# mLSTM gate exponentials for the queries, split into a rounded and a remaining part

## The chip, the cores and the metric

The kernel runs on one core of one Trainium2 chip. The metric is the device time of one execution in microseconds (us), the median of a few runs of the same program. Engines are called as the profile calls them: PE (TensorE matmuls), PEld (TensorE weight loads), DVE (VectorE), ACT (ScalarE), POOL (GpSimd), SP (SyncE, which starts DMAs here).

## The reference, cut to what matters

One step of two trunk layers of a streaming encoder for 512 prompt frames and 8 streams of 16 frames. In each layer an FFN, three parallel token mixers (MLA attention, mLSTM, HGRN2), an output projection and another FFN follow one another. The change touches the mLSTM, of which this is the part that counts:

```python
def step(carry, inp):                       # one chunk of L frames, 4 heads
    c, n, m = carry
    qc, kc, vc, lic, lfc = inp
    b = jnp.cumsum(lfc, axis=1)
    ...
    log_inter = b + m[:, None, :]
    m_t = jnp.maximum(log_inter, jnp.max(logw, axis=2))
    w_intra = jnp.exp(logw - m_t[:, :, None, :])
    w_inter = jnp.exp(log_inter - m_t)
    qk = jnp.einsum('bthd,bshd->btsh', qc, kc) * w_intra
    num = jnp.einsum('btsh,bshv->bthv', qk, vc) + w_inter[..., None] * jnp.einsum('bthd,bhdv->bthv', qc, c)
```

`w_inter` is one number for each head and frame, and it scales the queries `qc` of that head. All inputs and outputs are float32.

## The kernel before

The 640 frames (512 and 8 x 16) lie along the free dimension, as five tiles of 128 (`TILES` 5; tiles 0 to 3 are the prompt, `PT_` is 4). Each layer runs the FFN, the projection, `mla`, `recurrent`, `wout` and the second FFN. Every engine has its own program, written out by hand in the order in which it runs; waits on semaphores join them. Nothing is scheduled by a program: what stands earlier in an engine's code runs earlier.

**The attention loop (`mla`)** runs over 32 steps, n = 4 h + i, of 8 heads h and 4 query blocks i. In a step PE multiplies scores (L1157), DVE sets the masked corner and takes the maximum (`maximum(n)`: L2675, L2676), ACT takes the exponential with that maximum (`probabilities(n)`), PE transposes the result (L1166), ACT copies it back, and PE multiplies with the values (L1176). Scores run two steps ahead, so `maximum(21)` is needed by ACT's exponential of step 21, and that by PE's transpose of step 21. Between the steps each engine does other work of the layer:

- DVE computes the mLSTM gates of the 4 heads, on 4 partitions by 640 frames, one function ahead of the maximum of each of steps 5 and 8 to 16. `gate_starts_exponents` (step 14) leaves the logarithm of `w_inter` in `UB[0:4, 0, :]`. `gate_negative` (step 16) writes `NBR`, 64 rows high: it sets 64 rows to zero (L2766), writes the negated maximum, rounded to the type fp32r, into rows 0 to 3 (L2767), and what the rounding left into rows 32 to 35 (L2768). At step 20 DVE also multiplies a pair of heads' output (`pair_output`, L2688), after `maximum(20)`.
- ACT takes the gate exponentials at step 17 (`gates_exp`, L1936 to L1943), the last of them in place in `UB[0:4, 0, :]`, and then raises `ge_sb`. All of ACT's activations are recorded on line L1539, the helper.
- POOL works through the taps of the convolution (`tap_of`): two multiplications (L3216, L3217, one input from SBUF each) and an addition (L3219, two inputs from SBUF), over and over. After the taps it clears `QPE` and stores two states from `GB`; ACT waits for these stores ahead of `stream_keys(0)`.

After the loop PE runs `pair_rows` (L1187) and a few filling matmuls (L869), waits for ACT's `kn_sb`, and begins the attention of the streams (L1226). There ACT turns constants into fp32r for the mLSTM (`MASKR`, `SELR`, `IDR`, event `mr_sb`).

**The recurrent part (`recurrent`)** runs `front(t)` for the five tiles, each between the output and update products of earlier tiles. `front` multiplies masks and gate rows (L1336, L1338), queries with keys (L1351), transposes the keys of two head pairs g (L1354) and, for t = 1 to 4, spreads the four rows of `w_inter` over the 128 rows of a head pair: `SELG[:, g, :]` holds ones at the rows that belong together, and the product (L1356) is made in plain float32 with all 128 rows of `SELG` and of `UB[:, 0, cut]`. DVE then reads bank 1 of PSUM for the weighted keys `KW` (L2900) and bank 2 for the weighted queries `QG` (L2906).

Of the kernel before, what the change touches and what calls it, by code (L numbers as in the profile page):

```python
# [119 lines left out]
def shape_constants():  # L120

    inv = (10000.0 ** (-np.arange(0, ROPE, 2, dtype=np.float32) / ROPE)).astype(np.float32)
    pos = np.concatenate([np.arange(TP), np.tile(PAST + np.arange(TS), NSEQ)]).astype(np.float32)
    ang = inv[:, None] * pos[None, :]
    rope = np.concatenate([np.cos(ang)] * 2 + [-np.sin(ang), np.sin(ang)]).astype(np.float32)
    swap = np.zeros((P, P + ROPE), np.float32)
    for j in range(ROPE):
        swap[NOPE + (j + ROPE // 2) % ROPE, QK + j] = 1.0
        swap[[NOPE + j, QK + j], P + j] = 1.0
    s, t = np.arange(P)[:, None], np.arange(P)[None, :]  # L130
    causal = np.where(s <= t, 0.0, -FAR)
    streams = np.where((s <= t) & (s // TS == t // TS), 0.0, -FAR)
    masks = np.stack([causal, streams], axis=1).astype(np.float32)
    level = np.zeros((P, NLEV, P), np.float32)
    for n, h in enumerate(LEVELS):
        level[:, n] = (s // (2 * h) == t // (2 * h)) & (s % (2 * h) < h) & (t % (2 * h) >= h)
    level[:, NLEV - 1] = s == t
    starts = np.zeros(T, bool)
    starts[0:TP:P] = True
    starts[TP::TS] = True  # L140
    going = np.broadcast_to(1.0 - starts.astype(np.float32), (P, T))
    drop = np.zeros((MH, T), np.float32)
    drop[:, TP::TS] = -FAR
    select = np.zeros((P, MH, P), np.float32)
    for h in range(MH):
        select[[h, 32 + h], h] = 1.0
    pair = np.zeros((P, 2, P), np.float32)
    for h in range(MH):
        pair[h, h // 2, 64 * (h % 2):64 * (h % 2) + 64] = 1.0
    owner = (np.arange(P)[:, None] // TS == np.arange(NSEQ)[None, :]).astype(np.float32)  # L150
    return {"c_rope": rope, "c_swap": swap, "c_mask": masks, "c_level": level.astype(np.uint8),
            "c_going": np.ascontiguousarray(going), "c_drop": drop, "c_select": select, "c_pair": pair, "c_owner": owner,
            "c_ident": np.eye(P, dtype=np.float32), "c_ones": np.ones((P, P), np.float32)}
# [35 lines left out]
def encoder(nc, A, O):  # L189
# [51 lines left out]
    LVL = tile(ctx, "lvl", [P, NLEV, P], U8)  # L241
    AT = tile(ctx, "at", [P, TILES, 2, 2, P])
    QK1 = tile(ctx, "qk1", [P, 2, T])
    SELG = tile(ctx, "selg", [P, 2, P])
    GB = tile(ctx, "gb", [P, 2, T])
    s_w = ExitStack()
    tile(s_w, "gap_nbr", [P, T])
    NBR = tile(s_w, "nbr", [P, T], F32R)
    s_w.close()
    UB = tile(ctx, "ub", [P, 2, T])  # L250
# [215 lines left out]
    ext_sb, conv_sb, csilu_sb = event("ext_sb", 1), event("conv_sb", 2), event("csilu_sb", 2)  # L466
    tap_sb = event("tap_sb", 4)
    ga_sb, gl_sb, ge_sb, gt_sb = steps("gates_act", 4)
    gab_sb, gd_sb = steps("gates_dve", 2)
    gt_ps, oexp_sb, msk_sb = (event(n, 1) for n in ("gt_ps", "oexp_sb", "msk_sb"))  # L470
    mr_sb, qm_sb, cd_sb, sd_sb = (event(n, 1) for n in ("mr_sb", "qm_sb", "cd_sb", "sd_sb"))
    qg_sb = event("qg_sb", TILES - 1)
# [261 lines left out]
    def _(pe):  # L734
# [592 lines left out]
        def recurrent(l):  # L1327

            def front(t):
                cut = slice(t * P, (t + 1) * P)  # L1330
                if t:
                    pe.wait_ge(*wexp_sb.nth(l, t - 1))
                else:
                    pe.wait_ge(*mr_sb.nth(l, 0))
                mask = MASKR[:, t // PT_, :].unsqueeze(1).broadcast_to([P, MH, P])
                pe.matmul(PS[:, 0, :], IDR[:, :], mask, start=True, stop=False, skip_group_check=True)  # L1336
                for h in range(MH):
                    mm = pe.matmul(PS[:, 0, h * P:(h + 1) * P], SELR[0:64, h, :], NBR[0:64, cut],  # L1338
                                   start=False, stop=True, skip_group_check=True)
                mm.then_inc(nb_ps.sem, 1)  # L1340
                if t == 0:
                    pe.wait_ge(*csilu_sb.nth(l, 1))
                    pe.wait_ge(*spt_sb.nth(l, NSEQ - 1))
                else:
                    pe.wait_ge(*wt_sb.nth(l, t - 1))
                    pe.wait_ge(*kw_sb.nth(l, t - 1))
                    if t >= 2:
                        pe.wait_ge(*qg_sb.nth(l, t - 2))
                for h in range(MH):
                    rows = slice(64 * (h % 2), 64 * (h % 2) + 64)  # L1350
                    pe.matmul(PS[:, 1 + h % 2, h // 2 * P:h // 2 * P + P], QKC[rows, 2 + h // 2, cut],  # L1351
                              QKC[rows, h // 2, cut], start=True, stop=True)
                for g in range(2):
                    pe.transpose(PS[:, 1, 256 + g * P:256 + (g + 1) * P], QKC[:, 2 + g, cut], IDENT[:, :])  # L1354
                    if t:
                        pe.matmul(PS[:, 2, 256 + g * P:256 + (g + 1) * P], SELG[:, g, :], UB[:, 0, cut],  # L1356
                                  start=True, stop=True)
                if t:
                    pe.wait_ge(*kdt_sb.nth(l, t - 1))
                else:  # L1360
                    pe.wait_ge(*kd_sb.nth(l, 1))
                    pe.wait_ge(*mla_done.nth(l, 0))
                for g in range(2):
                    mm = pe.transpose(PS[:, 3, g * P:(g + 1) * P], KDF[:, g, cut], IDENT[:, :])
                mm.then_inc(mk_ps.sem, 1)
# [169 lines left out]
    def _(act):  # L1535
# [337 lines left out]
        def mla(l):  # L1873
# [62 lines left out]
            def gates_exp():  # L1936
                act.wait_ge(*gd_sb.nth(l, 0))
                act.wait_ge(*ml_zero.nth(l, 0))
                run(G3[64:68, :], GB[0:MH, 0, :], ACT.Exp, scale=-1.0)
                run(G3[96:100, :], GB[0:MH, 1, :], ACT.Exp)  # L1940
                run(WIE[:, 0:PT_], UB[0:MH, 0, ENDS_P], ACT.Exp)
                chain.link(run(WIE[:, PT_:12], UB[0:MH, 0, ENDS_S], ACT.Exp))
                run(UB[0:MH, 0, :], UB[0:MH, 0, :], ACT.Exp).then_inc(ge_sb.sem, 1)  # L1943

            def gate_columns():
                act.wait_ge(*gt_ps.nth(l, 0))
# [82 lines left out]
            for b in range(NSEQ):  # L2029
                if b + 2 < NSEQ:  # L2030
                    stream_keys(b + 2)
                if 1 <= b <= 3:
                    decays(l, b + 3)
                if b + 1 < NSEQ:
                    stream_transposed(b + 1)
                if b + 2 < NSEQ:
                    stream_exp(b + 2)
                if b == 0:
                    act.wait_ge(ml_in, 16 + (l + 1) * 64)
                    run(MASKR[:, :, :], MASK[:, :, :], ACT.Copy)  # L2040
                    run(SELR[:, :, :], SEL[:, :, :], ACT.Copy)
                    run(IDR[:, :], IDENT[:, :], ACT.Copy).then_inc(mr_sb.sem, 1)
                if b == 4:
                    act.wait_ge(*conv_sb.nth(l, 1))
                    run(QE[:, :, :], BC[:, :, :], ACT.Exp)
                if b == 5:
                    act.wait_ge(*kd_sb.nth(l, 0))
                    run(KDF[:, :, :], KDF[:, :, :], ACT.Exp)
                    run(EBL[:, :, 0:PT_], BC[:, :, ENDS_P], ACT.Exp)
                    run(EBL[:, :, PT_:12], BC[:, :, ENDS_S], ACT.Exp).then_inc(qe_sb.sem, 1)  # L2050
# [158 lines left out]
    def _(dve):  # L2209
# [450 lines left out]
        def mla(l):  # L2660
# [99 lines left out]
            def gate_ends_exponents():  # L2760
                for cut, n0, n1, w in GATE_CUTS:
                    rows = lambda ap: ap.rearrange("h (n t) -> h n t", t=w)
                    V.tensor_tensor(rows(GB[0:MH, 1, cut]), rows(G3[0:MH, cut]), spread(GE[:, n0:n1], w), ALU.subtract)

            def gate_negative():
                chain.link(V.memset(NBR[0:64, :].bitcast(F32), 0.0))  # L2766
                chain.link(V.tensor_scalar(NBR[0:MH, :], g, -1.0, None, ALU.mult))  # L2767
                V.scalar_tensor_tensor(out=NBR[32:32 + MH, :], in0=g, scalar=-1.0, in1=NBR[0:MH, :].bitcast(F32),  # L2768
                                       op0=ALU.mult, op1=ALU.subtract).then_inc(gd_sb.sem, 1)
# [12 lines left out]
            for n in range(NT):  # L2782
# [19 lines left out]
                    gate_ends_exponents()  # L2802
                if n == 16:
                    gate_negative()
                if n % PT_ == PT_ - 1 and n // PT_ + 1 < H:
                    rotated(n // PT_ + 1, 1)
                maximum(n)
# [76 lines left out]
        def recurrent(l):  # L2884
            dve.wait_ge(*gt_sb.nth(l, 0))

            def weights(t):
# [10 lines left out]
                if t >= 2:  # L2898
                    dve.wait_ge(*upd_ps.nth(l, t - 2))
                V.scalar_tensor_tensor(out=KW[:, t % 2, :, :],  # L2900
                                       in0=PS[:, 1, 256:512].rearrange("p (h d) -> p h d", d=DK),
                                       scalar=DK ** -0.5, in1=spread(GT[:, t, 96:100], DK),
                                       op0=ALU.mult, op1=ALU.mult).then_inc(kw_sb.sem, 1)
                if t:
                    cut = slice(t * P, (t + 1) * P)
                    V.tensor_tensor(QG[:, :, cut], PS[:, 2, 256:512].rearrange("p (g t) -> p g t", t=P),  # L2906
                                    QKC[:, 0:2, cut], ALU.mult).then_inc(qg_sb.sem, 1)

            def mlstm_out(t):
# [417 lines left out]
```

## Time and profile before

| | us |
|---|---|
| median of 3 runs | 2605.98 (2605.72 to 2606.77) |
| the profiled execution, its own time | 2605.07 |
| its span, first to last instruction | 2603.3 |
| PE busy | 2562.1 (98%) |
| DVE busy | 1637.9 (63%) |
| ACT busy | 1145.4 (44%) |
| POOL busy | 533.4 (20%) |

Between the span and the execution's own time lie 1.77 us, outside the instructions. The granted TensorE clock is 0.999 of full speed over the span. The stages that the change touches lie, in layer 0, at 617 to 706 us (attention loop), 706 to 764 us (attention of the streams) and 764 to 804 us (recurrent), and in layer 1 some 1283 us later. The chain of waits, followed back from the last instruction, tells which engine's work the end waits for at each moment; the timeline shows what each engine does at that time and how long it stood idle before.

### The profile page before, as it was taken

The numbers are of one execution on the slowest core, as the hardware profiler recorded it, in microseconds if no ns is written. First come the engines' busy times: TensorE is split into PE (matmuls) and PEld (weight loads), VectorE is DVE, ScalarE is ACT, GpSimd is POOL, SyncE is SP. The second block draws the span as 40 slices with busy tenths as digits, with TensorE's granted clock in tenths as the row PEclk, the third lists the DMA queues.
The fourth block names the chain that finished last, engine by engine and source line by source line (L and its number), as shares of the span: only waits on it lengthen the run. The fifth ranks groups of instructions, "written<-read, shape, count | busy, mean of one in ns | idle before, by whom it ended". The sixth has DMA issues, their size and how long they took to land.

```text
span 2603.3 us, 44569 instructions
## 1 busy us (share of the span) xinstructions
PE 2562.1 (98%) x17872; PEld 2446.5 (94%) x17872; DVE 1637.9 (63%) x2534; ACT 1145.4 (44%) x1946; POOL 533.4 (20%) x440
## 2 busy tenths in 40 slices
PE   9999999999999999999999999999999999999998
PEld 8999999996689999999999999999956899999998
DVE  5666575646465866657577574765564757757473
ACT  5343344424654534334454342553165635434253
POOL 0010112103754101011210110121066441101011
PEclk9999999999999999999999999999999999999999
DMA  3322324220025122332313222334000261322321
GB/s 116 90 81 81 97 65 113 73 59 11 20 54 100 49 82 81 85 94 71 108 33 97 82 71 76 88 90 105 27 11 29 46 130 33 97 81 71 88 83 59
DMA packets 369794, 190.73 MB, mean 73 GB/s; under 512 B 38541, under 2 KB 365536, under 8 KB 369630
## 3 DMA queue, kind: packets, MB, share of 16 engines
q1 hardware_dynamic: 365248, 177.89, 25.3%
q0 software_dynamic: 4000, 10.47, 1.7%
q8 instruction: 108, 1.77, 0.3%
q14 instruction: 56, 0.46, 0.1%
q10 hardware_dynamic: 382, 0.14, 0.0%
HBM read 182.53 MB, written 5.93 MB: 72 GB/s over the span
## 4 chain that ended last, share of the span: by engine, by line
PE 91%; DVE 3%; POOL 2%; ACT 2%; issue 1%; DMA 1%; SPq 0%; DVEq 0%; POOLq 0%; ACTq 0%
PE ps L737 27%; PE ps L739 27%; PE ps L738 27%; PE ps L1114 2%; POOL misc L3216 1%; POOL qkc L3219 1%; PE ps L1125 1%; PE ps L1226 1%; DVE at L2711 1%; PE ps L1227 1%; PE ps L1157 0%; PE ps L1248 0%; ACT css L1539 0%; PE ps L1176 0%; PE ps L1239 0%
## 5 line engine op out<-in xcount | busy, mean ns | idle before, releaser
L737 PE MATMUL ps<-xh,w 128*128 128x320 f32 x1920 | 595.1, 310 | 3.1 <-DVE css L2976 3.1
L739 PE MATMUL ps<-xh,w 128*128 128x320 f32 x1920 | 593.3, 309 | 0.0
L738 PE MATMUL ps<-xl,w 128*128 128x320 f32 x1920 | 593.2, 309 | 0.0
L1539 ACT ACTIVATE w<-raw 128x512 fp32r<-128x512 f32 (+3 forms) x372 | 315.8, 861 | 483.9 <-PE ps L739 466.2
L3073 POOL TENSOR_TENSOR hl<-ub,hh 128x640 fp32r<-128x640 f32 x88 | 174.2, 1980 | 1448.1 <-ACT hh L1539 1380.9
L737 PE MATMUL ps<-hh,w 128*128 128x320 f32 x1408 | 438.0, 311 | 3.3 <-DVE ub L2367 1.2
L739 PE MATMUL ps<-hh,w 128*128 128x320 f32 x1408 | 435.0, 309 | 0.0
L738 PE MATMUL ps<-hl,w 128*128 128x320 f32 x1408 | 435.0, 309 | 0.0
L737 PEld LDWEIGHTS ps<-xh,w 128*128 128x128 f32 x1920 | 360.4, 188 | 5.3 <-DVE css L2976 3.6
L738 PEld LDWEIGHTS ps<-xl,w 128*128 128x128 f32 x1920 | 360.4, 188 | 0.3
L739 PEld LDWEIGHTS ps<-xh,w 128*128 128x128 f32 x1920 | 360.4, 188 | 0.0
L737 PEld LDWEIGHTS ps<-hh,w 128*128 128x128 f32 x1408 | 264.2, 188 | 8.4 <-issue 8.0
L737 PE MATMUL ps<-tc,w 128*128 128x320 f32 x864 | 267.0, 309 | 0.0
L738 PE MATMUL ps<-tc,w 128*128 128x320 f32 x864 | 267.0, 309 | 0.0
L739 PE MATMUL ps<-tc,w 128*128 128x320 f32 x864 | 267.0, 309 | 0.0
L738 PEld LDWEIGHTS ps<-hl,w 128*128 128x128 f32 x1408 | 264.3, 188 | 0.5
L739 PEld LDWEIGHTS ps<-hh,w 128*128 128x128 f32 x1408 | 264.3, 188 | 0.0
L2378 DVE TENSOR_TENSOR y<-ps,y 128x640 f32<-128x640 f32 x83 | 68.4, 824 | 261.9 <-PE ps L739 261.9
L2242 DVE TENSOR_TENSOR w<-raw,w 128x512 fp32r<-128x512 f32 (+1 forms) x216 | 180.4, 863 | 3.9 <-ACT w L1539 3.9
L739 PEld LDWEIGHTS ps<-tc,w 128*128 128x128 f32 x864 | 162.2, 188 | 0.0
L737 PEld LDWEIGHTS ps<-tc,w 128*128 128x128 f32 x864 | 162.2, 188 | 0.0
L738 PEld LDWEIGHTS ps<-tc,w 128*128 128x128 f32 x864 | 162.2, 188 | 0.0
(420 smaller groups left out, 4674.4 us busy)
## 6 DMA issues: line engine op xcount, KB each, us to landing
raw<-in_w_ffn_in_dram SPq DMA_DIRECT2D x176, 512.0 KB
raw<-in_w_ffn_out_dram SPq DMA_DIRECT2D x192, 192.0 KB
raw<-in_w_in_dram SPq DMA_DIRECT2D x38, 512.0 KB
raw<-in_w_ffn_out_dram SPq DMA_DIRECT2D x64, 128.0 KB
wraw<-in_w_out_dram SPq DMA_DIRECT2D x8, 512.0 KB
raw<-in_w_out_dram SPq DMA_DIRECT2D x8, 512.0 KB
out_dram<-xio SPq DMA_DIRECT2D x5, 512.0 KB
xin<-in_x_prompt_dram SPq DMA_DIRECT2D x4, 512.0 KB, 7.6
```

The source lines that it names most:

```text
L737: pe.matmul(out, wh, xh, start=first, stop=False, skip_group_check=loose)
L738: pe.matmul(out, wh, xl, start=False, stop=False, skip_group_check=loose)
L739: return pe.matmul(out, wl, xh, start=False, stop=last, skip_group_check=loose)
L1114: mm = pe.matmul(PS[:, 6 + h % 2, at:at + w], k_, q_, start=True, stop=True)
L1125: mm = pe.matmul(PS[:, half, 0:HALF], WUQ[:, c, h, :], CQ[:, c, half * HALF:(half + 1) * HALF], start=c == 0, stop=c == 1)
L1226: pe.matmul(PS[:, 4, :], ql, CT[:, b % 2, :], start=True, stop=False)
L1227: pe.matmul(PS[:, 4, :], qp, KPT[:, b % 2, 0:PAST], start=False, stop=True)
L1539: return nc.scalar.activation(out, in_, func, **kw)
L2242: V.tensor_tensor(lo, group_raw(n, q % 2), hi.bitcast(F32), ALU.subtract)\
L2378: ins = V.tensor_tensor(y, ps, y, ALU.add) if add else V.tensor_copy(y, ps)
L2711: ins = V.copy_predicated(out, mask, new)
L3073: G.tensor_tensor(HL[:, k, :], UB[:, j, :], HH[:, k, :].bitcast(F32), ALU.subtract).then_inc(hl_ready.sem, 1)
```

## The change

The spread of `w_inter` is made from two parts in fp32r instead of from one row in float32. The exponential goes to `R[0:4, :]` instead of in place. A new function on DVE, `gate_parts`, stands ahead of the maximum of step 21: it waits for ACT's exponentials, clears 64 rows of `UBR` (which lies on the same memory as `UB[:, 0, :]`), writes the rounded exponential into rows 0 to 3 and the remaining part into rows 32 to 35. ACT makes an fp32r copy of `SELG` (in place), beside the other constants. `SELG` has ones at rows h and 32 + h. PE multiplies 64 rows of `SELGR` with 64 rows of `UBR`, both heads' products ahead of the two key transposes, into bank 1; the transposes go to bank 2, and DVE reads the two banks accordingly. At tile 1 PE waits for `gx_sb`, which `gate_parts` raises.

```diff
@@ shape_constants
-        pair[h, h // 2, 64 * (h % 2):64 * (h % 2) + 64] = 1.0
+        pair[[h, 32 + h], h // 2, 64 * (h % 2):64 * (h % 2) + 64] = 1.0
@@ encoder, tiles
+    s_w = ExitStack()
+    SELGR = tile(s_w, "selgr", [P, 2, P], F32R)
+    s_w.close()
     SELG = tile(ctx, "selg", [P, 2, P])
     GB = tile(ctx, "gb", [P, 2, T])
     s_w = ExitStack()
-    tile(s_w, "gap_nbr", [P, T])
+    UBR = tile(s_w, "ubr", [P, T], F32R)
     NBR = tile(s_w, "nbr", [P, T], F32R)
     s_w.close()
-    gab_sb, gd_sb = steps("gates_dve", 2)
+    gab_sb, gd_sb, gx_sb = steps("gates_dve", 3)
@@ PE, front(t)
+                if t == 1:
+                    pe.wait_ge(*gx_sb.nth(l, 0))
+                for g in range(2 if t else 0):
+                    pe.matmul(PS[:, 1, 256 + g * P:256 + (g + 1) * P], SELGR[0:64, g, :], UBR[0:64, cut],
+                              start=True, stop=True)
                 for g in range(2):
-                    pe.transpose(PS[:, 1, 256 + g * P:256 + (g + 1) * P], QKC[:, 2 + g, cut], IDENT[:, :])
-                    if t:
-                        pe.matmul(PS[:, 2, 256 + g * P:256 + (g + 1) * P], SELG[:, g, :], UB[:, 0, cut],
-                                  start=True, stop=True)
+                    pe.transpose(PS[:, 2, 256 + g * P:256 + (g + 1) * P], QKC[:, 2 + g, cut], IDENT[:, :])
@@ ACT, gates_exp
-                run(UB[0:MH, 0, :], UB[0:MH, 0, :], ACT.Exp).then_inc(ge_sb.sem, 1)
+                run(R[0:MH, :], UB[0:MH, 0, :], ACT.Exp).then_inc(ge_sb.sem, 1)
@@ ACT, attention of the streams, b == 0
                     run(SELR[:, :, :], SEL[:, :, :], ACT.Copy)
+                    run(SELGR[:, :, :], SELG[:, :, :], ACT.Copy)
@@ DVE, mla
+            def gate_parts():
+                dve.wait_ge(*ge_sb.nth(l, 0))
+                chain.link(V.memset(UBR[0:64, :].bitcast(F32), 0.0))
+                chain.link(V.tensor_copy(UBR[0:MH, :], R[0:MH, :]))
+                V.tensor_tensor(UBR[32:32 + MH, :], R[0:MH, :], UBR[0:MH, :].bitcast(F32), ALU.subtract)\
+                    .then_inc(gx_sb.sem, 1)
@@ DVE, loop over the steps
+                if n == 21:
+                    gate_parts()
                 maximum(n)
@@ DVE, recurrent, weights(t)
-                                       in0=PS[:, 1, 256:512].rearrange("p (h d) -> p h d", d=DK),
+                                       in0=PS[:, 2, 256:512].rearrange("p (h d) -> p h d", d=DK),
-                    V.tensor_tensor(QG[:, :, cut], PS[:, 2, 256:512].rearrange("p (g t) -> p g t", t=P),
+                    V.tensor_tensor(QG[:, :, cut], PS[:, 1, 256:512].rearrange("p (g t) -> p g t", t=P),
```

`chain.link` lets DVE wait until the instruction before has finished.

The order of the instructions moves at two places. On PE, in `front(1)` of layer 0 (`qkc` are queries and keys, `kdf` the decayed keys of the HGRN2), this stands in a row before:

```order
L1351 MATMUL ps<-qkc 128x128 x4
L1354 MATMUL ps<-ident,qkc 128x128
L1356 MATMUL ps<-ub,selg 128x128
L1354 MATMUL ps<-ident,qkc 128x128
L1356 MATMUL ps<-ub,selg 128x128
L1364 MATMUL ps<-ident,kdf 128x128 x2
```

And this in the changed kernel, whose line numbers are a few higher:

```order
L1354 MATMUL ps<-qkc 128x128 x4
L1359 MATMUL ps<-ubr,selgr 128x128 x2
L1362 MATMUL ps<-ident,qkc 128x128 x2
L1369 MATMUL ps<-ident,kdf 128x128 x2
L1393 MATMUL ps<-va,wt 128x65 x4
```

The two spreading products now stand together, directly behind the products of queries and keys, and the two key transposes together behind them.

On DVE, in the attention loop of layer 0, from the pair output of step 20 on (`y` is the pair's output, `mx` the maxima), this stands before:

```order
L2688 TENSOR_TENSOR y<-ps,y 128x512
L2675 MEMSET ps 64x64
L2676 TENSOR_REDUCE mx<-ps 128x1
L2675 MEMSET ps 64x64
L2676 TENSOR_REDUCE mx<-ps 128x1
```

And this in the changed kernel:

```order
L2694 TENSOR_TENSOR y<-ps,y 128x512
L2773 MEMSET ubr 64x640
L2774 CAST ubr<-r 4x640
L2775 TENSOR_TENSOR ubr<-r,ubr 4x640
L2681 MEMSET ps 64x64
L2682 TENSOR_REDUCE mx<-ps 128x1
```

The three instructions of `gate_parts` stand between the pair output and the maximum of step 21.

## Rows read from the trace of the kernel before

**Rows 1.** The page: busy time of PE, and the chain by engine.
```profile
PE 2562.1 (98%) x17872; PEld 2446.5 (94%) x17872; DVE 1637.9 (63%) x2534; ACT 1145.4 (44%) x1946; POOL 533.4 (20%) x440
...
PE 91%; DVE 3%; POOL 2%; ACT 2%; issue 1%; DMA 1%; SPq 0%; DVEq 0%; POOLq 0%; ACTq 0%
```

**Rows 2.** Chain in order of time, front(3), layer 0: start us, us, what.
```profile
779.21 0.26 PE ps L1354
779.47 0.22 PE ps L1356 x2
779.69 0.11 PE ps L1354
779.80 0.22 PE ps L1356 x2
780.02 0.22 PE ps L1364 x2
```

**Rows 3.** Chain in order of time, steps 20 and 21, layer 0.
```profile
671.87 0.69 DVE y L2688
...
672.56 0.12 DVE ps L2675
...
673.79 0.44 PE ps L1166 x2
```

**Rows 4.** Timeline of PEld, front(2), layer 0: start, us, line, operands, [idle before].
```profile
772.12 0.41 PEld L1338 LDWEIGHTS ps<-nbr,selr 64*128 64x128 f32 x3 [0.24 <-issue]
...
772.45 0.19 PEld L1338 LDWEIGHTS ps<-nbr,selr 64*128 64x128 f32 x1
```

**Rows 5.** Timeline of DVE and POOL at step 16, layer 0.
```profile
657.00 1.54 POOL L3219 TENSOR_TENSOR qkc<-qkc,misc 128x640 f32<-128x640 f32 x1
...
657.10 0.69 DVE L2676 TENSOR_REDUCE mx<-ps 128x1 f32<-128x512 f32 x1
...
657.86 0.59 DVE L2766 MEMSET nbr<- 64x640 f32 x1
...
658.49 0.48 DVE L2767 TENSOR_SCALAR nbr<-r 4x640 fp32r<-4x640 f32 x1
...
658.74 1.36 POOL L3234 TENSOR_TENSOR dd<-hf 128x640 f32<-128x640 f32 x1 [0.20 <-POOL qkc L3219]
...
659.01 1.77 DVE L2768 SCALAR_TENSOR_TENSOR nbr<-r,nbr 4x640 fp32r<-4x640 f32 x1
```

**Rows 6.** Timeline of POOL, step 9, layer 0.
```profile
639.90 2.74 POOL L3216 TENSOR_SCALAR misc<-extp,par 128x512 f32<-128x512 f32 x1
```

**Rows 7.** Timeline of DVE, step 10, layer 0.
```profile
641.93 0.76 DVE L2734 TENSOR_TENSOR g<-gb,ub 4x640 f32<-4x640 f32 x1
```

**Rows 8.** Timeline of ACT and POOL, steps 20 and 21, layer 0.
```profile
669.72 0.73 ACT L1539 ACTIVATE ub<-ub 4x640 f32<-4x640 f32 x1
...
671.99 1.54 POOL L3219 TENSOR_TENSOR qkc<-qkc,misc 128x640 f32<-128x640 f32 x1
...
673.62 1.57 POOL L3216 TENSOR_SCALAR misc<-extp,par 128x512 f32<-128x512 f32 x1
```

**Rows 9.** Timeline of steps 20 and 21, layer 1: POOL and DVE.
```profile
1954.89 1.54 POOL L3219 TENSOR_TENSOR qkc<-qkc,misc 128x640 f32<-128x640 f32 x1
...
1955.11 0.11 DVE L2675 MEMSET ps<- 64x64 f32 x1
```

**Rows 10.** Timeline of PE, end of the attention loop, layer 0.
```profile
699.31 1.04 PE L1187 MATMUL ps<-ident,rs 128*64 128x128 f32 x16
...
700.82 1.05 PE L1226 MATMUL ps<-ct,qlat 128*128 128x512 f32 x2
```

**Rows 11.** The same of layer 1.
```profile
1981.85 1.04 PE L1187 MATMUL ps<-ident,rs 128*64 128x128 f32 x16
...
1983.59 1.12 PE L1226 MATMUL ps<-ct,qlat 128*128 128x512 f32 x2
```

**Rows 12.** Timeline of ACT, attention of the streams, layer 0.
```profile
716.72 0.41 ACT L1539 ACTIVATE maskr<-mask 128x256 fp32r<-128x256 f32 x1
...
718.51 0.60 ACT L1539 ACTIVATE ct<-ps 128x512 f32<-128x512 f32 x1 [0.67 <-PE ps L1216]
```

## The prediction

> **What bounds the kernel now.** I read the page first. PE is busy in 98% of the span, and the chain followed back from the last instruction lies on PE for 91% of it [rows 1]. So a matmul saved on PE is worth its full time wherever the chain is on PE, and work on DVE, busy 63% [rows 1], is free wherever PE does not wait for it. Both have to be looked up where the change puts them, since the share of busy time says nothing of a single place. The chain in order of time shows the recurrent part: the transposes and the spreading products of `front` stand in the chain one behind the other [rows 2], and so they do at all eight tiles that have a spreading product (four in each layer). The same view at steps 20 and 21 of the attention loop shows the other place: there the chain is on DVE. It runs through the pair output, then the corner and the maximum of step 21, and from there over ACT's exponential to PE's transposes at 673.79 [rows 3]. That is exactly the gap into which `gate_parts` is put.
>
> **The products (removed work).** A float32 product of 128 columns is two records in the trace, 0.22 us together, 0.11 us each [rows 2]. What a one-pass product costs, the trace shows directly: the rows of `NBR` are spread by fp32r products of the same form (64 rows, 128 columns, L1338), one record each. Three of them start from 772.12 on and the fourth at 772.45, so one takes (772.45 - 772.12) / 3 = 0.11 us [rows 4]. The saving is 0.11 us a product, 2 x 0.11 = 0.22 us a tile, and over 4 tiles and 2 layers 8 x 0.22 = **1.76 us**. The two transposes stay at 0.26 and 0.11 us: the first one behind 64-row products costs more than the second [rows 2], and after the change it still stands behind 64-row products. The bounds: nothing, if a product here costs as much as now, and 8 x 0.28 = 2.2 us, if the first product, on rows 0 to 63, overlaps with the last query-key product, on rows 64 to 127, by half a record. I take 1.76, since L1338 is the same form.
>
> The new wait at tile 1 is for an event of the attention loop, one whole stage back. A wait that is long over shows at most as an idle 0.24 us of the weight loads [rows 4], beside a matmul that still runs; I put it at nothing, at worst 2 x 0.24 us. Behind it on PE stands the rest of `front(1)`, and DVE's weights wait for that.
>
> **The three instructions on DVE (added work).** Their likeness stands in the trace: `gate_negative` has a memset of the same 64 x 640, a conversion of the same 4 x 640, and a third one of the same size [rows 5]. The memset takes 0.59 us and begins 0.07 us behind the reduction before it (657.10 + 0.69, 657.86); each link between two of them costs 0.04. The other two depend on POOL. The conversion began at 658.49, while POOL's addition ran until 657.00 + 1.54 = 658.54, and ended at 658.97: it took 0.43 once POOL was done. The third began at 659.01 and took 1.77 us, with POOL's L3234 (two inputs from SBUF) running until 660.10: it took 0.68 once that was done [rows 5]. So DVE's instructions that need both SBUF ports stand still while a POOL instruction with two SBUF inputs runs. A POOL instruction with one SBUF input, L3216, ran from 639.90 until 642.64 [rows 6], and DVE's subtraction of 4 x 640 from 641.93 took 0.76 us under it [rows 7], the size of a plain pass. So I let a subtraction run freely beside L3216.
>
> Nothing moves ahead of step 21, hence POOL's place is known. **Layer 0**: the exponential ends at 670.45 [rows 8], so `ge_sb` is no wait. The pair output ends at 672.56 [rows 3]. Memset 672.63 to 673.22; conversion issued at 673.26, held by POOL's addition until 671.99 + 1.54 = 673.53 [rows 8], done at 673.96; POOL's L3216, due at 673.62 [rows 8], now starts behind it; subtraction 674.00 to 674.76. The corner of step 21 begins at 674.77 in place of 672.56: **2.21 us** later. Queued behind it on DVE are the maxima of steps 21 and 22; ACT's exponentials wait for them and PE's transposes for these, with no other work in front of them on PE. **Layer 1**: the corner began at 1955.11, and POOL's addition runs until 1954.89 + 1.54 = 1956.43 [rows 9]. Memset until 1955.77, conversion held until 1956.43 and done at 1956.86, subtraction until 1957.66: 1957.67 in place of 1955.11, **2.56 us** later.
>
> Does PE win this back before the loop ends? In layer 0 the streams' scores begin 700.82 - 699.31 = 1.51 us after `pair_rows` [rows 10], back to back. In layer 1 it is 1983.59 - 1981.85 = 1.74 us [rows 11]: there PE waits 0.23 us for ACT and the stores behind POOL's taps. So layer 1 gives 0.23 us back. POOL's own chain gets later too, by the 0.34 us for which the conversion holds L3216, but stays ahead of PE's by more than a us. Exposed: 2.21 + 2.56 - 0.23 = **4.54 us**. The bounds for the pair of delays: without any hold by POOL 0.07 + 0.59 + 0.04 + 0.43 + 0.04 + 0.76 + 0.01 = 1.94 us a layer, so 2 x 1.94 - 0.23 = 3.65; with the subtraction held as well, 7.44 (the second rival below); nothing, if the delay were covered (the first).
>
> **Edits at nothing.** The exponential into `R` has the same size as the one in place. ACT's copy of `SELG` has the size of the copy of `MASK`, 0.41 us, and ACT stands idle 0.67 us right behind these copies [rows 12]; without that cover it would cost 2 x 0.41. The exchanged PSUM banks change no form on DVE.
>
> **Sum.** 4.54 - 1.76 = +2.78 us. The profiled execution goes from 2605.07 to 2607.85; it lies 0.91 under the median of the runs shown, and the median goes from 2605.98 to **2608.8 us**, 0.1% more.
>
> **Rivals.**
>
> *The delay is covered.* DVE is idle 37% of the span, and if something else ended the attention loop last, only the products would count: 2605.98 - 1.76 = 2604.2 us. Against it: the chain shows PE's transposes waiting for just this maximum [rows 3], and PE runs back to back at the loop's end in layer 0 [rows 10]. Covered in one layer alone, it would give 2606.5.
>
> *The subtraction is held too (slower).* If DVE's subtraction, which has two inputs in SBUF, must let POOL's L3216 finish first, it begins 1.57 us after the conversion's end [rows 8] and takes 0.68 more, as L2768 did [rows 5]. Layer 0: 673.96 + 1.57 + 0.68 + 0.01 = 676.22, a delay of 3.66. Layer 1: 1956.86 + 1.57 + 0.68 + 0.01 = 1959.12, a delay of 4.01. Together 3.66 + 4.01 - 0.23 - 1.76 = +5.68: 2611.7 us. It is past 0.2% once the holds exceed 2.4 us in sum, that is when both subtractions wait out nearly a whole L3216. For it: L2768 waited so for L3234. Against it: L2734 ran unhindered under L3216 [rows 6, 7]. The Trainium skill, "SBUF — State Buffer", section "Who interferes with whom", states this rival as its rule: an instruction of VectorE with two SBUF inputs contends with a GpSimd instruction that reads SBUF, and who comes first blocks the other for the whole instruction. By that rule the time is 2611.7; the rows of L3234 agree with it, the row of L2734 does not.
>
> *The products gain nothing* (the one-pass product with its weights takes two records' time here): +4.54, 2610.5 us. Against it stands the spacing of L1338 [rows 4].
>
> **How the numbers follow.** The forecast has 0.72; the subtraction held 0.12; the delay covered 0.08, half of it in one layer alone; the products without gain 0.05; 0.03 are left for what I don't see, such as a TensorE clock that falls because PE stands still some 2 us longer in each loop (it is 0.999 over the span now). About 0.2%, 5.2 us, is what a measurement of this kernel can tell from no change: faster means under 2600.8, slower over 2611.2. The forecast, the covered delay and the products without gain are all within it. Slower takes the held subtraction and most of the rest, 0.13; faster has no case and keeps 0.02; the same 0.85. The range reaches down to a delay covered in one layer, 2605.2 with half a us for the scatter of runs and the overlap of products, and up to the held subtraction, 2612.0.
>
> **What would show it.** In the profile after: the spreading products as one record each with 0.11 us in the chain, and a recurrent part shorter by 0.88 us a layer; three new DVE instructions between the pair output and the corner of step 21, with a conversion of about 0.7 and 1.05 us and a subtraction of 0.76; PE's transposes of step 21 some 2.2 us later against the steps before, and the streams' scores later by 2.2 and 2.3. A subtraction of 2.2 us shows the held one; a loop that ends no later shows the covered delay. The forecast is wrong if PE finds other work in that gap, or if the clock shows less than full speed behind it.

## The result, and the profile after

The changed kernel takes 2610.89 us (median of 20 runs, 2609.38 to 2616.73) beside 2606.86 us of the kernel before (20 runs, 2605.17 to 2608.98): a ratio of 1.0017, 95% interval 1.0012 to 1.0023. That is 4.0 us more. The forecast was 2.8 us more, and no change beyond 0.2%. Three terms were mis-sized (the products, the conversion and the subtraction), and one cause that I had kept 0.03 for came in.

**The products.** The chain of waits of the changed kernel, `front(3)` of layer 0 (start, us, what; L1359 is the spreading product, L1362 the transpose):

```profile
782.84 0.17 PE ps L1359 x2
783.02 0.37 PE ps L1362 x2
```

0.54 us for the four instructions, where [rows 2] show 0.26 + 0.22 + 0.11 + 0.22 = 0.81. That is 0.27 us a tile, and 8 x 0.27 = 2.2 us, the far bound of the term. No idle time stands in the chain ahead of L1359, at tile 1 either.

**The three instructions of `gate_parts`.** DVE in layer 0, timeline (start, us, line, operands, idle before):

```profile
671.92 0.69 DVE L2694 TENSOR_TENSOR y<-ps,y 128x512 f32<-128x512 f32 x1 [3.57 <-ACT y L1544]
672.69 0.59 DVE L2773 MEMSET ubr<- 64x640 f32 x1
673.32 0.59 DVE L2774 CAST ubr<-r 4x640 fp32r<-4x640 f32 x1
673.94 1.20 DVE L2775 TENSOR_TENSOR ubr<-r,ubr 4x640 fp32r<-4x640 f32 x1
675.15 0.11 DVE L2681 MEMSET ps<- 64x64 f32 x1
```

POOL at that time, its multiplication with one SBUF input:

```profile
673.66 1.68 POOL L3231 TENSOR_SCALAR misc<-extp,par 128x512 f32<-128x512 f32 x1
```

The corner of step 21 begins 675.15 - 672.62 = 2.53 us later than it would behind the pair output, not 2.21. The conversion took 0.59 us (about 0.70 forecast), but the subtraction 1.20 in place of 0.76. In layer 1 the conversion and the subtraction read:

```profile
1958.23 0.95 DVE L2774 CAST ubr<-r 4x640 fp32r<-4x640 f32 x1
1959.21 1.19 DVE L2775 TENSOR_TENSOR ubr<-r,ubr 4x640 fp32r<-4x640 f32 x1
```

The delay there is 2.89 us (forecast 2.56).

**PE behind it.** Timeline of PE, the transposes of step 21 in the two layers:

```profile
676.37 0.44 PE L1169 MATMUL ps<-ident,pb 128*128 128x128 f32 x2 [2.67 <-ACT pb L1544]
1961.64 0.44 PE L1169 MATMUL ps<-ident,pb 128*128 128x128 f32 x2 [2.67 <-ACT pb L1544]
```

PE stands idle 2.67 us in each. The windows of layer 0 right behind it (columns: window, length, PE busy and count, granted clock, DMA share, GB/s):

```profile
677.00:679.00 2.00, 2.00 (x8) 0.51 0.00 0
679.00:681.00 2.00, 2.00 (x6) 0.64 0.01 4
681.00:683.00 2.00, 2.00 (x17) 1.00 0.00 0
```

0.51 is the lower level of the clock, 1.2 GHz; PE had been idle for 2.67 us and had worked again for less than one us at 2.4 GHz when it fell. The chain of the same kernel shows what that costs:

```profile
676.37 0.44 PE ps L1169 x2
...
677.18 2.43 PE ps L1128 x4
679.61 1.34 PE ps L1160 x2
...
688.11 0.22 PE ps L1169 x2
```

The last row is the transposes of step 25. From those of step 21 on they come after 11.74 us. In the kernel before, layer 0, they begin at 683.89, 10.10 us behind the 673.79 of [rows 3]. So the lower clock took 1.64 us. In layer 1 of the same execution the windows behind the same idle 2.67 us show 1.00, and the way takes 1971.74 - 1961.64 = 10.10 us: no fall there.

**The sum.** The chain in order of time, at the start of the last stage and in its last row, in the kernel before:

```profile
2582.66 0.89 PE ps L830 x8
...
2589.18 4.36 PE ps L830 x24
```

and after:

```profile
2586.66 0.89 PE ps L833 x8
...
2594.22 4.96 PE ps L833 x24
```

Up to that stage the changed kernel is 2586.66 - 2582.66 = 4.00 us behind. The terms: delays 2.53 + 2.89, less the 0.23 that layer 1 gives back, +5.19; products -2.2; the clock in layer 0 +1.64; and -0.6 between the layers, where the execution of the kernel before has a wait of PE for POOL (0.4 us on L769, and a slower start of PE behind it). Three of the eleven other profiled executions, all with the change in some form, show that wait too and eight do not, so I don't count it as the change's. Together the terms come to +4.03. In the last stage the two executions differ by another 12.52 - 10.88 = 1.64 us at a granted clock below 1.00; that stage varies between executions of one kernel too (12.32 us in one of e1_end), and I leave it out.

### The profile page after: what moved, and what is told of

It is laid out like the page before. It is cut to its first block, busy times and chain, and to the rows that moved or that the text cites. A ratio compares the mean times of both kernels' runs of the same rounds, so it can differ in the third digit from the quotient of the medians.

```text
span 2608.9 us, 44545 instructions
## 1 busy us (share of the span) xinstructions
PE 2562.5 (98%) x17856; PEld 2447.0 (94%) x17856; DVE 1642.7 (63%) x2540; ACT 1145.2 (44%) x1948; POOL 532.4 (20%) x440
## 4 chain that ended last, share of the span: by engine, by line
PE 93%; DVE 4%; ACT 2%; issue 1%; DMA 0%; SPq 0%; DVEq 0%; ACTq 0%
PE ps L740 27%; PE ps L742 27%; PE ps L741 27%; PE ps L1117 2%; PE ps L1128 1%; PE ps L1160 1%; PE ps L1179 1%; PE ps L1229 1%; DVE at L2717 1%; PE ps L1230 1%; PE ps L1169 1%; DVE mx L2682 0%; PE ps L1251 0%; ACT css L1544 0%; PE ps L1242 0%
```

## The experiments

All ratios are to the kernel before on the same chip, with a 95% interval. Theory A: the change loses by the delay at step 21 and by the clock behind it, and wins by the products' one pass. The rivals put the loss into PE's own instructions, or the gain into something else than the pass.

**1. The same work at another place.** `e1_end`:

```diff
-                if n == 21:
-                    gate_parts()
...
             (ahead of the last pair_output, behind the last inverse sums)
+            gate_parts()
```

> gate_parts is moved from step 21 to the end of the attention loop, between the last inverse sums and the last pair output, where DVE stands idle for over 5 us waiting for ACT's copy. Theory A (the changed kernel loses on DVE at step 21, 2.53 and 2.89 us, and by the lower clock behind PE's idle 2.67 us in layer 0, and wins 0.27 us a tile on the products): both losses go, the products stay, 8 x 0.27 = 2.2 us under the kernel before, a ratio of 0.9992; PE's wait ahead of the transposes of step 21 is no longer than before, and the granted clock stays at 1.00 behind it. Rival B (the loss is in the products' new order, the new wait on PE or ACT's additional copy): the place of gate_parts is of no matter, and the ratio stays near 1.0017.

Measured: 2602.84 us, 0.9989 (0.9980 to 0.9998). DVE at the end of the loop, layer 0:

```profile
696.40 0.59 DVE L2773 MEMSET ubr<- 64x640 f32 x1
697.03 0.48 DVE L2774 CAST ubr<-r 4x640 fp32r<-4x640 f32 x1
697.54 0.81 DVE L2775 TENSOR_TENSOR ubr<-r,ubr 4x640 fp32r<-4x640 f32 x1
701.80 0.69 DVE L2694 TENSOR_TENSOR y<-ps,y 128x512 f32<-128x512 f32 x1 [3.44 <-ACT y L1544]
```

Behind the subtraction DVE still waits 3.44 us for ACT, so nothing is delayed, and the transposes of step 21 stand without idle time before them (674.12 in layer 0). Nothing else was moved: the whole loss of the change lies in the place of `gate_parts`. Beside an idle POOL the three instructions take 0.59, 0.48 and 0.81 us, so what POOL adds to the subtraction at step 21 is 1.20 - 0.81 = 0.39 us.

A second series, `e1_again`:

> The kernel of e1_end once more, on the chip of e8_behind. Theory A: 8 x 0.27 = 2.2 us under the kernel before, a ratio of 0.9989 to 0.9994, and no fall of the granted clock in either attention loop, since PE stands no longer idle there than in the kernel before. Rival: the 0.9989 of the first series was a chance of its executions, and the ratio is 0.9996 or more.

Measured: 2603.89 us beside 2607.15, again 0.9989 (0.9980 to 0.9998), and a granted clock of 1.00 over both attention loops. This version beats both kernels, the one before by 0.11%: 3 us, of which the products account for 2.2; the rest lies inside the interval.

**2. One pass against two.** `e2_f32` has the products of the changed kernel in plain float32; `e7_endf32` does the same to `e1_end`:

```diff
-  SELGR[0:64, g, :], UBR[0:64, cut],
+  SELGR[0:64, g, :].bitcast(F32), UBR[0:64, cut].bitcast(F32),
```

> The changed kernel with its spreading products in plain float32 (the same 64 rows, the same order, the same gate_parts at step 21). Theory A: each product is two records again, 16 x 0.11 = 1.8 us more than the changed kernel, about 6.3 us more than the kernel before, a ratio of 1.0024. Rival B (one pass gains nothing, it is the new order or the height of 64 rows that shortens the recurrent part): no more than the changed kernel, 1.0017, and 0.54 us in the chain for products and transposes of a tile.

> gate_parts at the end of the attention loop as in e1_end, with the products in plain float32, all else as there. Theory A (the whole gain is the one pass): the products and transposes of a tile take 0.82 us in the chain in place of 0.54, as in e2_f32, and 8 x 0.27 = 2.2 us are lost against e1_end; the time is that of the kernel before, a ratio of 0.9998 to 1.0000. Rival (the gain of e1_end has another source too): it stays below the kernel before, 0.9995 or less.

Measured: `e2_f32` 2614.76 us, 1.0032 (1.0020 to 1.0044); `e7_endf32` 2606.54 us, 1.0000 (0.9991 to 1.0009). The chain of `e7_endf32`, `front(3)`:

```profile
779.59 0.45 PE ps L1359 x4
780.03 0.37 PE ps L1362 x2
```

Four records and 0.82 us, the 0.81 of the kernel before; so in float32 neither 64 rows in place of 128 nor the new order gains anything: the 0.27 us a tile come with the one pass. With it taken away and the place of `gate_parts` mended, the time is that of the kernel before. `e2_f32` lies 0.0015 or 3.9 us above the changed kernel, more than the 1.8 expected: 2.2 are the pass by its chain, and the rest lies within the two intervals. Its profiled execution, the slowest of the six, shows the fall of the clock in both layers (below), where that of the changed kernel has one.

**3. The order of the products.** `e6_order` is `e1_end` with transpose, product, transpose, product, as in the kernel before. `e8_behind` has both products behind both transposes:

```diff
@@ e6_order
-                for g in range(2 if t else 0):
-                    (product g)
                 for g in range(2):
                     (transpose g)
+                    if t:
+                        (product g)
@@ e8_behind
-                for g in range(2 if t else 0):
-                    (product g)
                 for g in range(2):
                     (transpose g)
+                for g in range(2 if t else 0):
+                    (product g)
```

> gate_parts at the end of the attention loop as in e1_end, and on PE the old order: transpose, product, transpose, product. Theory A (one pass is worth 0.11 us a product, and the rest of the 0.27 us a tile comes from the products standing behind 64-row products, where the first two overlap): the four instructions take 0.59 to 0.65 us in the chain of waits in place of 0.54, 8 x 0.05 to 0.11 = 0.4 to 0.9 us more than e1_end, a ratio of 0.9991 to 0.9993. Rival (the order is of no matter): 0.54 us and 0.9989.

Measured: 2610.19 us, 1.0020 (1.0012 to 1.0029). I had expected 0.4 to 0.9 us more than `e1_end`; it is several us more. The chain of `e6_order`, `front(3)` (L1359 the transposes, L1361 the products, L1369 the next transposes):

```profile
780.16 0.26 PE ps L1359
780.42 0.26 PE ps L1361
780.68 0.26 PE ps L1359
780.94 0.25 PE ps L1361
781.19 0.37 PE ps L1369 x2
```

and of `e1_end` (L1359 the products, L1362 the transposes):

```profile
779.18 0.17 PE ps L1359 x2
779.35 0.37 PE ps L1362 x2
779.72 0.22 PE ps L1369 x2
```

Each instruction that follows one of the other height (128 rows behind 64, or 64 behind 128) takes 0.26 us in place of 0.11. `e6_order` has five such changes a tile, `e1_end` one: 1.40 against 0.76 us, and 8 x 0.64 = 5.1 us in sum. The spans of the profiled executions differ by 5.3 (2607.5 and 2602.2). The ratios differ by 0.0031, 8 us, with intervals that leave room for the 5.1. Four of the twelve executions of `e6_order` took 2615.4 to 2618.0 us, at a mean granted clock of 0.995 or 0.996, and no execution of `e1_end` is above 2606.1 or below 0.997; so part of the rest may be the clock, which no trace of those four shows. From these rows came the expectation of the next kernel:

> e1_end with the two one-pass products behind the two transposes. Theory A (an instruction whose weights have another height than those before it, 64 rows behind 128 or 128 behind 64, starts its successor 0.15 us later, 0.26 in place of 0.11 us): three changes of height a tile in place of one, and the overlap of the first two products lost; transposes 0.37, products 0.37, and L1369 behind them 0.37 in place of 0.22 us: 0.35 us a tile more than e1_end, 8 x 0.35 = 2.8 us in sum, a ratio near 1.0000. Rival (only an alternation as in e6_order is dear, or the time is lost elsewhere): 0.54 and 0.22 us as in e1_end, and its ratio.

Measured: 2607.28 us, 1.0002 (0.9993 to 1.0011), and its chain, `front(3)` (L1359 transposes, L1361 products):

```profile
780.98 0.37 PE ps L1359 x2
781.35 0.37 PE ps L1361 x2
781.71 0.37 PE ps L1369 x2
```

1.11 us against 0.76: the 0.35 a tile that three changes of height and the lost short pair had been put at, and 0.0013 in the ratio, 3.4 us for an expected 2.8. The type of the products is not what costs: behind the float32 products of 64 rows in `e7_endf32` the two transposes take the same 0.37 us, and behind float32 products of 128 rows the second transpose of [rows 2] takes 0.11. The Trainium skill, "TensorEngine Tiling (Array Packing)", section "Key Properties", says that changing the tiling mode, and not just the tile, drains TensorE. The rows agree, and price one change at 0.26 - 0.11 = 0.15 us here.

**4. The clock behind the idle time.** `e3_spin` gives PE filling matmuls while it waits, `e0_again` is the changed kernel once more:

```diff
@@ e3_spin, PE, ahead of the transposes of step 21
+                if n == 20:
+                    pe.wait_ge(*pt_sb.nth(l, n))
+                    held(pe)
+                    spin(PS[:, 5, :], 8)
```

> The changed kernel with eight filling matmuls on PE ahead of the transposes of step 21, in the time in which PE stood idle 2.67 us. gate_parts stays at step 21. Theory A: PE's waiting is short, the granted clock stays at 1.00 behind it in both layers, and the 1.65 us that layer 0 lost between the transposes of step 21 and the streams' scores are not lost: 0 to 1.6 us less than the changed kernel, since not every execution need have the fall, a ratio of 1.0012 to 1.0016, with the runs closer together. Rival B (these 1.65 us come from something else than the clock, or the filling matmuls delay the transposes): 1.0017 or more.

> The changed kernel once more, beside the other runs of this group. Theory A (the fall of the granted clock behind PE's idle 2.67 us at step 21 comes in some executions and some layers): this execution again stands idle 2.67 us in both layers, while the falls need not be the same as in the first one (layer 0 alone); where there is none, the way from the transposes of step 21 to the streams' scores takes 27.0 us, where there is one, about 28.7. Rival (the fall belongs to layer 0 and to what PE does there): again layer 0 alone. The ratio is 1.0017 as before.

Measured: `e3_spin` 2608.73 us, 1.0011 (1.0002 to 1.0020); `e0_again` 2611.03 us, 1.0021 (1.0012 to 1.0030). PE in `e3_spin`, layer 0, and the windows behind:

```profile
676.63 0.44 PE L1169 MATMUL ps<-ident,pb 128*128 128x128 f32 x2 [0.95 <-ACT pb L1548]
```

```profile
677.00:679.00 2.00, 2.00 (x11) 1.00 0.00 0
679.00:681.00 2.00, 2.00 (x16) 1.00 0.02 4
```

In `e0_again` the transposes of layer 1 are slow themselves, and the clock stays low for several us:

```profile
1964.20 0.69 PE L1169 MATMUL ps<-ident,pb 128*128 128x128 f32 x2 [2.69 <-ACT pb L1544]
```

```profile
1964.00:1966.00 2.00, 1.80 (x7) 0.50 0.00 0
1966.00:1968.00 2.00, 2.00 (x5) 0.50 0.00 0
1968.00:1970.00 2.00, 2.00 (x5) 0.50 0.00 0
```

The way from the transposes of step 21 to those of step 25, from the chains of all executions in which PE stood idle for 2.67 us or more (`e5_between` is told of below), and of three in which it did not (a dash: the chain does not pass there):

| | idle of PE, us | layer 0, us | layer 1, us |
|---|---|---|---|
| changed kernel | 2.67 | 11.74 | 10.10 |
| e0_again | 2.69 | 11.78 | 12.99 |
| e2_f32 | 2.68 | 11.59 | 13.04 |
| e5_between | 3.07, 3.08 | 10.10 | 11.74 |
| e3_spin | 0.95, 0.93 | 10.10 | 10.10 |
| e1_end | none | 10.09 | 9.89 |
| before | none | 10.10 | - |

So the clock fell behind six of eight such idle stretches, in either layer, at a cost of 1.5 to 2.9 us each, and behind neither of the two short ones of `e3_spin`. These are four executions, two of them (`e0_again`, `e2_f32`) the slowest of their series, so the count is no rate. The rival (that it belongs to layer 0) is out. By the time alone the case would not be made, since the intervals of `e3_spin` and of the changed kernel overlap; the granted clock in the rows makes it. What decides which of two equal idle stretches is followed by a fall, these runs don't tell. The length alone does not: at the end of the recurrent part of layer 1, PE stands idle 1.72 or 1.73 us in five executions, and behind that the clock fell in three of them (`e0_again`, `e4_n20`, `e5_between`) and stayed at 1.00 in two (the changed kernel, `e8_behind`). In `e8_behind` it is 0.50 from 770 to 772 us, in the recurrent part of layer 0, with no idle stretch of PE of 0.9 us or more in that part before it.

**5. One place earlier.** `e4_n20` puts `gate_parts` ahead of the pair output of step 20:

```diff
-                if n == 21:
-                    gate_parts()
...
+                if n == 20:
+                    gate_parts()
```

> gate_parts stands one place earlier, ahead of the pair output of step 20, where DVE is idle from 668.3 to 671.9 us; ACT's exponentials are done at 670.45, so 1.4 of its 2.5 us are covered. Theory A (only what is not covered delays PE): the pair output comes 0.6 to 1.0 us later in each layer, PE stands idle 0.6 to 1.1 us in place of 2.67, the clock stays at 1.00, and the sum is -2.2 + 1.2 to 2.0: a ratio of 0.9996 to 0.9999. Rival B (the loss is not this delay): 1.0017.

Measured: 2604.73 us, 0.9996 (0.9987 to 1.0005). PE at step 21 of layer 0:

```profile
674.75 0.44 PE L1169 MATMUL ps<-ident,pb 128*128 128x128 f32 x2 [0.95 <-ACT pb L1544]
```

From the transposes of step 20 to those of step 21 it takes 2.79 us in both layers; in `e1_end` 1.98 and 1.67, in the changed kernel 4.50 in both. So 0.8 and 1.1 us of the delay are left, the clock stays at 1.00 in both loops, and the time stands between the two others, where these 1.9 us and the products put it.

**6. What POOL holds.** `e5_between` splits the clearing:

```diff
-                chain.link(V.memset(UBR[0:64, :].bitcast(F32), 0.0))
+                chain.link(V.memset(UBR[0:32, :].bitcast(F32), 0.0))
                 chain.link(V.tensor_copy(UBR[0:MH, :], R[0:MH, :]))
+                chain.link(V.memset(UBR[32:64, :].bitcast(F32), 0.0))
```

> The changed kernel with the clearing of UBR in two halves: rows 0 to 31 ahead of the rounded part, rows 32 to 63 between the rounded and the remaining part. One more memset of 0.59 us with a link of 0.04 on DVE. The subtraction then is issued 0.63 us later, some 0.9 us into POOL's multiplication in place of 0.3. Theory A1 (POOL's multiplication with one SBUF input holds DVE's subtraction only in its first part): the subtraction falls from 1.20 to about 0.76 us, the delay of step 21 grows by only 0.2 us a layer, 0.4 in sum, ratio 1.0019. Rival (the subtraction is slow beside this multiplication all the time): it stays at 1.2 us, 0.63 us a layer more, 1.3 in sum, ratio 1.0022.

Measured: 2612.66 us, 1.0026 (1.0017 to 1.0036). The time decides nothing between the two; the rows do. DVE and POOL, layer 0:

```profile
674.30 0.59 DVE L2775 MEMSET ubr<- 32x640 f32 x1 [0.19 <-DVE ubr L2774]
674.93 0.81 DVE L2776 TENSOR_TENSOR ubr<-r,ubr 4x640 fp32r<-4x640 f32 x1
```

```profile
673.87 1.68 POOL L3232 TENSOR_SCALAR misc<-extp,par 128x512 f32<-128x512 f32 x1
```

Issued 674.93 - 673.87 = 1.06 us into POOL's multiplication, the subtraction takes 0.81 us, its time beside an idle POOL; issued 673.94 - 673.66 = 0.28 us into it, 1.20. So this multiplication slows it early and not later on. In `e4_n20` the subtraction, issued 0.55 us into POOL's shorter multiplication (L3232, 128x128), took 0.82. There it was POOL that lost time: L3232, started together with the conversion, took 0.91 us where it takes 0.60 otherwise, and the addition behind it, started under the subtraction, 1.78 in place of 1.54. Which part of the multiplication holds the subtraction stays open. The second memset began with 0.19 us of idle time that I had not counted, and the delay grew by 0.4 us a layer in place of 0.2.

## Why the prediction was right, and where its sizes were off

**The place of the loss** was right: the three instructions stand on the path at step 21, nothing on PE covers them, and the loop ends later by them. `e1_end` shows it, since the loss is gone with the place alone. The 0.23 us given back in layer 1 came as worked out: from the pair output to the streams' scores the lag grew by 2.66 = 2.89 - 0.23 us. That wait of 0.23 us is not in every execution, though: in `e1_end`, where nothing is delayed, the streams' scores of layer 1 begin 1.51 us after `pair_rows`, in `e1_again` 1.81, where [rows 11] have 1.74.

**The subtraction** was the mis-sized term of the added work: 1.20 us in place of the 0.76 read from L2734 [rows 7]. Both stand under POOL's multiplication; but L2734 began 2 us into a long one [rows 6], and L2775 0.28 us into a short one. The long one took 2.74 us, where the same form takes 1.57 in [rows 8], and an earlier DVE instruction (L2730, 639.60 to 641.25) lay over its first part. I had carried the row over without looking at how far the other engine was, or at why it took so long. With the conversion 0.1 us shorter than forecast in each layer, the delays came to 5.42 in place of 4.77 us, +0.65. Nor did the conversion hold POOL's L3216 back by the 0.34 us worked out: as L3231 it began at 673.66, 0.10 us behind POOL's addition as usual, and took 1.68 us in place of 1.57.

**The rival of the held subtraction** did not come in as written: the subtraction ended at 673.94 + 1.20 = 675.14, and POOL's L3231 ran until 673.66 + 1.68 = 675.34. By the rule of the Trainium skill, "SBUF — State Buffer", section "Who interferes with whom", it would have waited for that end. The trace disagrees for this pair: a hold of 0.39 us, not of the instruction. For POOL's addition with two SBUF inputs the rows go on agreeing: the conversion ended 0.35 us after that addition in layer 0 and 0.34 us after it in layer 1, where it took 0.95 us, and it took 0.48 where POOL was idle.

**The products** saved 2.2 us, the upper bound, and not the 1.76 taken: 0.54 us a tile in place of 0.59. A pair takes 0.17 us in the chain, not 0.22. The reason that I had named for that bound, an overlap of the first product with the last query-key product on the other 64 rows, shows in PE's timeline of `front(3)` (L1354 is queries with keys), in the changed kernel:

```profile
782.18 0.66 PE L1354 MATMUL ps<-qkc 64*128 64x128 f32 x7
782.60 0.41 PE L1359 MATMUL ps<-ubr,selgr 64*128 64x128 f32 x2
```

and in `e7_endf32`:

```profile
778.93 0.66 PE L1354 MATMUL ps<-qkc 64*128 64x128 f32 x7
779.43 0.61 PE L1359 MATMUL ps<-ubr,selgr 64*128 64x128 f32 x4
```

The one-pass product starts 0.42 us behind the first of these seven records, the float32 product 0.50 us. Of the 0.08 us, 0.05 are left in the chain (0.17 in place of 0.22). In `e8_behind`, where the pair stands behind the transposes, it takes 0.37 - 0.15 = 0.22 us. Why the float32 product does not start early in the same place stays open. That the transposes cost 0.26 and 0.11 us as before was right, for the reason given: they still stand behind 64-row products. What I had not seen is how much hung on it: in the old order the one-pass products would have lost by the changes of height more than they win (`e6_order`). The price stood in the trace of before, next to the row that I used: three of L1338, which have 64 rows and stand behind a product of 128, take 0.48 us in the chain of `front(3)`, not 3 x 0.11. The 0.24 us of idle weight loads in [rows 4], which I had read as what is left of a long past wait, stand before L1338 as well, and the code has no wait there; the new wait at tile 1 showed nothing.

**The clock** was in the 0.03 for what I did not see, and in the last sentence on what would make the forecast wrong. It fell behind six of eight idle stretches. With the two terms as measured, the forecast of +2.78 becomes 2.78 + 0.65 - 0.44 = +3.0 us. That the two errors nearly cancel is luck. `e3_spin`, in which the clock stays up, measures 0.0011, +2.9 us. The changed kernel's own two series, 0.0017 and 0.0021 (4.4 and 5.5 us), lie 1.5 to 2.6 us above that, which is what is left for the clock; the intervals overlap, so this share is an estimate from the medians.

**The edits at nothing** cost nothing. ACT's idle time ahead of `ct`, 0.67 us in [rows 12], is 0.36 after its additional copy, in both layers, and PE does not wait for it. The new wait on PE shows no idle time.

## What to carry to other kernels

An idle stretch of an engine is worth looking for a few steps further on: the same three instructions cost over 5 us ahead of one maximum and nothing where the engine waits for another one anyway. Where a delay leaves TensorE idle, its price is not the idle time alone; look at the granted clock behind it. A duration read beside another engine's instruction holds only for the same distance from that instruction's start.

## What the runs showed of the hardware that I had not expected

A change between products of 64 and of 128 rows costs TensorE 0.15 us each time, in either direction and also between products of one type (0.26 in place of 0.11 us for the instruction behind it), so that two one-pass products between two transposes take more time than the four float32 records they replace: 1.03 us for the four instructions of `e6_order` against 0.81 in [rows 2].

The granted clock fell to its lower level behind six of eight idle stretches of 2.67 to 3.08 us at step 21, three times before PE's first instruction and three times 0.7 to 1.5 us after it had begun again. Equal stretches in the same execution could be followed by a fall or by none, and three of five stretches of 1.72 to 1.73 us elsewhere were followed by one.

A one-pass product on rows 0 to 63 starts 0.08 us sooner behind a query-key product on rows 64 to 127 than a float32 product does in the same place, and keeps 0.05 us of it.
